# Latent attention and mLSTM of the odd layer: who computes the norms, in which order, and with which waits

## The reference, cut to what matters

```python
def odd_mixer(hn, positions, w_in, b_gate, g_qa, g_kva, w_q_up, w_kv_up, g_q, g_k, g_mh, w_out):
    z = hn @ w_in                       # 1024 -> 2216 columns
    q_lat, kv_lat, k_pe, mq, mk, mv, mo, mi, mf = jnp.split(z, ...)
    y_c = latent_attention(...)         # 8 heads, 64 content + 32 rotary columns, values 64
    h_m = mlstm_chunkwise(mq, mk, mv, mi + b_gate[:4], mf + b_gate[4:])   # 4 heads, 64, values 128
    y_d = sigmoid(mo) * rmsnorm(h_m, g_mh).reshape(...)
    return jnp.concatenate([y_c, y_d], -1) @ w_out

# in latent_attention: each head of q and of k is normed, content and rotary part separately
q = (rmsnorm(q_lat, g_qa) @ w_q_up);  kv = (rmsnorm(kv_lat, g_kva) @ w_kv_up)
q_nope = rmsnorm(q[..., :64], g_q[:64]); q_pe = rope(rmsnorm(q[..., 64:], g_q[64:]))
k_nope = rmsnorm(k_nope, g_k[:64]);      k_pe = rope(rmsnorm(k_pe, g_k[64:]))
```

## Time and profile before

| | |
|---|---|
| runs, us | 1380.41, 1379.68, 1378.28 (median 1379.68) |
| the profiled execution, us | 1380.87, its span 1379.0 |
| busy share of the span | PE 92%, DVE 55%, ACT 35%, POOL 2% |
| mean granted TensorE clock | 0.961 of 2.4 GHz |
| odd mixer | about 353 to 512 us of the span |

### The profile page before, as it was taken

How to read it: one execution, slowest core, us unless ns; L and a number is a source line. 1 busy time by engine, 2 the same in 40 slices (tenths; PEclk the granted TensorE clock), 3 DMA queues, 4 the chain that set the end, 5 groups by cost and what they waited for, 6 DMA issues and landing times.

```text
span 1379.0 us, 16368 instructions
## 1 busy us (share of the span) xinstructions
PE 1262.5 (92%) x6228; PEld 884.1 (64%) x6228; DVE 760.9 (55%) x1450; ACT 482.7 (35%) x806; POOL 27.0 (2%) x60
## 2 busy tenths in 40 slices
PE   6979999999896889999987998789999999999996
PEld 5967888876774667888875996554544454444442
DVE  5765877785657667777775998632122212222122
ACT  4424444444544335444444653411111111111111
POOL 0000000000000000000000300000000000000000
PEclk9989999999997689999999999889999999999999
DMA  8447766653421227777534320399999999999994
GB/s 272 149 153 287 268 244 244 243 183 137 169 95 51 92 87 285 267 254 254 194 110 150 122 77 1 150 424 418 414 432 427 429 432 431 431 429 429 432 430 186
DMA packets 113020, 354.42 MB, mean 257 GB/s; under 512 B 6762, under 2 KB 62755, under 8 KB 96578
## 3 DMA queue, kind: packets, MB, share of 16 engines
q1 hardware_dynamic: 106626, 328.48, 60.8%
q0 software_dynamic: 6336, 25.17, 4.6%
HBM read 352.58 MB, written 1.05 MB: 256 GB/s over the span
## 4 chain that ended last, share of the span: by engine, by line
PE 76%; DVE 10%; DMA 7%; ACT 3%; SPq 2%; issue 1%; DVEq 0%; ACTq 0%
PE ps L401 14%; PE ps L403 13%; PE ps L402 13%; PE ps L2538 13%; PE ps L2569 7%; PE ps L2527 4%; PE ps L2036 3%; DMA dense_weights<-in_moe_w_up 2%; DMA third_gate_up<-in_moe_w_up 2%; DMA second_expert<-in_moe_w_up 2%; DVE w_lo L375 1%; SPq L1053 1%; DMA dense_weights<-in_ev_w_in 1%; PE ps L2583 1%; PE ps L962 1%
## 5 line engine op out<-in xcount | busy, mean ns | idle before, releaser
L375 DVE TENSOR_TENSOR w_lo<-dense_weights,w_hi 128x1024 fp32r<-128x1024 f32 (+1 forms) x228 | 273.1, 1212 | 122.3 <-ACT w_hi L370 121.6
L370 ACT CAST w_hi<-dense_weights 128x1024 fp32r<-128x1024 f32 (+1 forms) x228 | 234.5, 1042 | 260.1 <-PE ps L403 236.3
L401 PE MATMUL ps<-w_hi,xT_lo 128*128 128x512 f32 (+1 forms) x624 | 251.1, 402 | 22.1 <-DVE xT_lo L2187 6.0
L403 PE MATMUL ps<-w_hi,xT_hi 128*128 128x512 f32 (+1 forms) x624 | 245.2, 393 | 0.0
L402 PE MATMUL ps<-w_lo,xT_hi 128*128 128x512 f32 (+1 forms) x624 | 245.1, 393 | 0.0
L401 PEld LDWEIGHTS ps<-w_hi,xT_lo 128*128 128x128 f32 x624 | 119.9, 192 | 51.1 <-issue 13.6
L403 PEld LDWEIGHTS ps<-w_hi,xT_hi 128*128 128x128 f32 x624 | 119.6, 192 | 25.4
L402 PEld LDWEIGHTS ps<-w_lo,xT_hi 128*128 128x128 f32 x624 | 120.2, 193 | 24.4 <-issue 0.7
L2676 DVE TENSOR_TENSOR hnT<-ps,g_bc 128x512 f32<-128x512 f32 x32 | 22.1, 692 | 163.5 <-PE ps L2569 163.5
L2685 DVE SCALAR_TENSOR_TENSOR cmask<-ge_th,ps 128x256 f32<-128x256 f32 x32 | 13.5, 422 | 163.0 <-ACT ge_th L2627 163.0
L2627 ACT ACTIVATE ge_th<-ps 128x256 f32<-128x256 f32 x32 | 12.3, 385 | 202.3 <-PE ps L2538 202.3
(11 more groups left out here) (404 smaller groups left out, 1778.0 us busy)
## 6 DMA issues: line engine op xcount, KB each, us to landing
ada_w<-in_ada_w POOLq DMA_DIRECT2D x12, 2048.0 KB, 12.2
dense_weights<-in_w_gate SPq DMA_DIRECT2D x22, 1024.0 KB, 7.1
dense_weights<-in_w_up SPq DMA_DIRECT2D x22, 1024.0 KB, 9.4
dense_weights<-in_w_down SPq DMA_DIRECT2D x22, 1024.0 KB, 5.0
dense_weights<-in_moe_w_gate SPq DMA_DIRECT2D x11, 2048.0 KB, 18.5
dense_weights<-in_moe_w_up SPq DMA_DIRECT2D x11, 2048.0 KB, 22.9
dense_weights<-in_moe_w_down SPq DMA_DIRECT2D x11, 2048.0 KB, 18.4
second_expert<-in_moe_w_gate SPq DMA_DIRECT2D x11, 2048.0 KB, 17.3
```

Of the source, the lines that this page charges most:

```text
L370: act.copy(split_view(w_hi, name, i, j), piece(name, i, j)).then_inc(hi_ready, 1)
L375: dve.tensor_tensor(split_view(w_lo, name, i, j), piece(name, i, j), split_view(w_hi, name, i, j).bitcast(F32), ALU.subtract).then_inc(pie ...
L401: pe.matmul(out, left[1], right[0], start=start, stop=False)
L403: return pe.matmul(out, left[0], right[0], start=False, stop=stop)
```

## The change

Nothing that is computed changes in the reference's sense; who does it, and when, does.

- Both barriers (`stage_end`, at the end of `OddHeads` and of `OddAttend`) are gone; named semaphores stand in for them (`act_copied`, `dve_copied`, `turned`).
- The factors of q and their multiplications move from after `scaled(4)` to before it (`q_factors`).
- Keys: ScalarE squares each quarter of kv out of PSUM with the factor 1/64 in its scale, and copies it; VectorE sums four quarters, takes one root, and multiplies once. The gain of the keys is applied when the turned keys are copied out, as a scale per partition (`gk_col`, made by three operations at the start of `OddIn`). ScalarE copies the rotary parts.
- TensorE turns the memory's q and k before it makes kv, and counts kv up by quarters.
- ScalarE loads the table for the exponential early, with a one-element operation.
- Gate sums: TensorE makes them between turned q and turned k, VectorE makes the columns before it copies turned keys.
- The mLSTM weights are made two operations after each of heads 4 to 7. The values' copy goes to ScalarE, the tanh before the last four copies.
- The turned attention half is moved into the last steps of `OddAttend`; the division has four operations instead of six; the mLSTM norm's squares are summed by ScalarE head by head; root and gate are applied in one operation per head and tile (eight).

```diff
@@ OddIn.dve
                 own(dve.tensor_tensor(g_k[:, 0:NOPE], g_k[:, 0:NOPE], g_q[:, 0:NOPE], ALU.mult))
+                wide = probT[:, 0, 0:QK]
+                own(dve.tensor_tensor(wide[:, 0:NOPE], ident[:, 0:NOPE], g_k[:, 0:NOPE], ALU.mult))
+                own(dve.tensor_copy(wide[:, NOPE:], ident[:, NOPE:QK]))
+                own(dve.tensor_reduce(gk_col, wide, AX.X, ALU.add))
                 self.up.turns_of(dve, own, self.freq)
...
                 split_upto(dve, split_lo, "od_in", 4, 3, 0)
+                odd_heads.q_factors(dve, own)
                 scaled(4)
@@ OddUp.act
+                act.wait_ge(self.mqk_turned, 1)
+                act.copy(mqkT[:], ps[:, 2:4, :].rearrange("p b (c s) -> p (b c) s", c=2)).then_inc(self.mqk_freed, 1)
...
-                act.wait_ge(up_used, 1)
-                act.copy(od_kv[:].rearrange("p t h d -> p t (h d)").rearrange("p t (a b) -> p (t a) b", a=2),
-                         ps[:, 4:8, :]).then_inc(self.kv_copied, 1)
...
+                for t in range(T):
+                    key = act.copy(od_k[:, t, :, NOPE:], od_z[:, t, AT_KPE:AT_KPE + ROPE].unsqueeze(1).to_broadcast([P, HEADS, ROPE]))
+                key.then_inc(self.exps, 1)
+                act.activation(turns[:, 0, 0:1], lf[:, 0, 0, 0:1], ACT.Exp)
+                for g in range(4):
+                    t, heads = g // 2, slice(g % 2 * (HEADS // 2), (g % 2 + 1) * (HEADS // 2))
+                    made = ps[:, 4 + g, :].rearrange("p (h d) -> p h d", h=HEADS // 2)
+                    act.wait_ge(up_used, g + 1)
+                    act.activation(od_k[:, t, heads, 0:NOPE], made[:, :, 0:NOPE], ACT.Square, scale=float(NOPE) ** -0.5
+                                   ).then_inc(self.kv_copied, 1)
+                    act.copy(od_kv[:, t, heads, :], made).then_inc(self.kv_copied, 1)
@@ OddHeads
+                for g in range(4):
+                    dve.wait_ge(self.up.kv_copied, 2 * g + 1)
...
+                    own(dve.tensor_reduce(ms[:, at:at + HEADS // 2], od_k[:, g // 2, half, 0:NOPE], AX.X, ALU.add))
+                rsqrt(dve, own, ms[:, cut], rs[:, cut], rtmp[:, 0, cut], rtmp[:, 1, cut])
+                dve.wait_ge(self.up.kv_copied, 8)
+                dve.tensor_tensor(k3[:, :, 0:NOPE], kv3[:, :, 0:NOPE], self.per_head(2 * n, NOPE), ALU.mult).then_inc(self.k_ready, 1)
+                odd_attend.gate_columns(dve, own)
...
+            def act(self, act):
+                for b in (0, 1, 2, 3, 5, 7):
+                    if b == 5:
+                        split_upto(act, split_hi, "od_out", 0, 3, ahead=0)
+                    act.wait_ge(self.turned, b + 1)
...
-                stage_end(pe)
@@ OddAttend
+                    if step == self.N:
+                        for b in range(2):
+                            odd_out.turn(pe, b)
...
+                    if hd >= HEADS - MH:
+                        memory_weights(hd - (HEADS - MH))
+                odd_out.gate(act)
                 for hd in range(HEADS, self.N):
                     copy(hd)
-                stage_end(act)
...
+                odd_out.gains(dve, own)
                 for m in range(MH):
+                    if m == 3:
+                        for b in range(2):
+                            odd_out.low(dve, b)
...
-                    own(dve.tensor_copy(den[:, 0], num[:, :, MV]))
-                    own(dve.tensor_scalar(den[:, 1], den[:, 0], -1.0, None, ALU.mult))
-                    own(dve.tensor_tensor(den[:, 0], den[:, 0], den[:, 1], ALU.max))
-                    own(dve.tensor_tensor(den[:, 0], den[:, 0], emt[:, :, m], ALU.max))
+                    own(dve.tensor_tensor(den[:, 0], num[:, :, MV], emt[:, :, m], ALU.max))
+                    own(dve.scalar_tensor_tensor(out=den[:, 0], in0=num[:, :, MV], scalar=-1.0, in1=den[:, 0], op0=ALU.mult, op1=ALU.max))
@@ OddOut
+                for m in range(MH):
+                    act.wait_ge(odd_attend.y_freed, T + m + 1)
+                    for t in range(T):
+                        act.activation(junk[:, t, m], y_d[:, t, m, :], ACT.Square, scale=float(MV) ** -0.5,
+                                       accum_out=ms[:, t * MH + m:t * MH + m + 1]).then_inc(self.tanh, 1)
...
+                for m in range(MH):
+                    for t in range(T):
+                        last = dve.scalar_tensor_tensor(out=y_d[:, t, m, :], in0=y_d[:, t, m, :], scalar=rs[:, t * MH + m:t * MH + m + 1],
+                                                        in1=g[:, t, m, :], op0=ALU.mult, op1=ALU.mult)
+                    if m % 2 == 1:
+                        last.then_inc(self.y, 1)
```

More of the change, by code:

```diff
@@ L1607, in dve @@
-                stage_end(dve)
-            def act(self, act):
-                for b in range(1, 8, 2):
-                    act.wait_ge(self.turned, b + 1)
-                    dst = (qT if b < 4 else kT)[0:QK, 2 * (b % 4):2 * (b % 4) + 2, :]
-                    act.copy(dst, ps[0:QK, b, :].rearrange("p (h s) -> p h s", h=2))
-                stage_end(act)
+                cut = slice(2 * n, 3 * n)
+                for g in range(4):
+                    dve.wait_ge(self.up.kv_copied, 2 * g + 1)
+                    at, half = 2 * n + g * (HEADS // 2), slice(g % 2 * (HEADS // 2), (g % 2 + 1) * (HEADS // 2))
+                    own(dve.tensor_reduce(ms[:, at:at + HEADS // 2], od_k[:, g // 2, half, 0:NOPE], AX.X, ALU.add))
@@ L1848, in act, with gate, gains @@
+            def gate(self, act):
+                act.activation(od_z[:, :, self.gains_at], od_z[:, :, AT_MO:AT_MI], ACT.Tanh, scale=0.5).then_inc(self.tanh, 1)
+            def gains(self, dve, own):
+                dve.wait_ge(self.tanh, 1)
+                g = od_z[:, :, self.gains_at]
+                own(dve.scalar_tensor_tensor(out=g, in0=g, scalar=1.0, in1=g_mh[:].unsqueeze(1).to_broadcast([P, T, MH * MV]),
+                                             op0=ALU.add, op1=ALU.mult))
             def act(self, act):
-                mo = od_z[:, :, AT_MO:AT_MI]
@@ L1891, in dve, with turn @@
                         ins.then_inc(h_ready, 1)
[L1893 to L1900 removed]
+            def turn(self, pe, b):
+                for c in (2 * b, 2 * b + 1):
+                    for t in range(T):
+                        at = (c % 2) * S + t * P
+                        last = pe.transpose(ps[:, b, at:at + P], mix[:, t, c * P:(c + 1) * P], ident[:])
+                last.then_inc(self.turned, 1)
+            def pe(self, pe):
                 def rest():
[L1904 to L1905 removed]
+                    for b in (2, 3):
+                        pe.wait_ge(self.y, b - 1)
+                        self.turn(pe, b)
                     pe.wait_ge(self.lo, 4)
[L1908 removed]
                 pe.wait_ge(self.lo, 2)
@@ L2820, in _ @@
             odd_in.pool(pool)
-            for _ in range(2):
-                stage_end(pool)
             ada_loads(pool, 1)
```

201 lines of the change are left out of this document (85 added, 116 removed).

## The result

The changed kernel takes 1371.26 us (median of 5, 1369.76 to 1371.75), the kernel before 1379.68 on the same chip (5, 1378.28 to 1381.89): ratio 0.9926, 95% interval 0.9908 to 0.9943: a gain under 1%, but the interval leaves out 1. The forecast was 1370.1 with a range of 1365.0 to 1375.0. The profiled execution took 1370.21 us, its span 1368.5, so 10.5 us less span than before.

What follows compares the result with a forecast made beforehand. It saw three bounds in turn: VectorE's and ScalarE's chain to the first exponential, a slow-TensorE head loop, a tail waiting for VectorE. Terms -0.8 + 5.4 + 0.7 + 2.2 + 1.2 + 0.9 = 9.6 us gave 1370.1, range 1365.0 to 1375.0.

Steps and rivals of the forecast that it cites:

- steps 1 and 4: Three new operations starting `OddIn`, 0.8 us lost; head 8's transposes to `OddOut`'s first product, 2.2 us saved.
- the second part of 3: From head 4's exponential to head 8's transposes: weights without a lump, 0.7 us saved, between -0.3 and 1.4.
- Start of `OddIn`: Three new VectorE operations lengthen TensorE's wait for piece 3's low part: 0.8 us lost, 0.6 to 1.9.
- Way to the first exponential: Query factors move into VectorE's idle time, VectorE then waits for ScalarE's squares: 5.4 us saved, 4.0 to 6.7.
- Heads: Nothing changes from the first exponential to head 4's; from there to head 8's transposes 0.7 us saved.
- End of the heads: From head 8's transposes to `OddOut`'s first product, 17.5 us becomes 15.2: 2.2 us saved, 1.5 to 4.
- The wait in the first block: TensorE's 1.19 us wait in `OddOut` for the gated half disappears: 1.2 us saved, at least 0.5.
- The clock: Shorter gaps around `OddOut` win back part of the 3.1 us lost to TensorE's lower clock: 0.9 us saved.
- Rival A: TensorE's clock stays down through all heads: 5.8 us saved, median 1373.9; chance 0.20.
- Rival B: The gap at 363 us grows, the clock stays down in `OddIn`: up to 9 us slower, 1388.5; chance 0.05.
- Rival C: The experts' weight stream, behind the odd mixer, swallows the gain: median 1379.5; chance 0.07.
- Rival D: The clock comes up in the heads: 14.3 us saved, median 1365.4; chance 0.08.

Runs made afterwards that it cites:

- e1: Changed kernel with the three operations that make the key gains' column moved from the start of `OddIn` to before the squares of q: 1366.08 us, ratio 0.990.
- e2: Changed kernel with the query factors put back behind the last scaled part, `scaled(4)`: 1369.48 us, ratio 0.9932.
- e3: Changed kernel with the one-element Exp that loads ScalarE's table moved from ahead of the key squares to behind the copy of `v_aug`: 1366.38 us, ratio 0.9895.
- e5: Changed kernel with unread TensorE transposes added ahead of the keys and through all heads: 1358.45 us, ratio 0.9842.
- e9: Kernel before the change with unread transposes added in all TensorE's waits in its heads and `OddOut`: 1370.15 us, ratio 0.9934.
- e11: The changed kernel run once more, unedited: 1368.21 us, ratio 0.9924.
- e8: Changed kernel with the mLSTM weights of the four memory heads made in one lump behind head 6's copy, as before the change: 1367.49 us, one run.
- e6: Changed kernel with `OddOut`'s normalisation back on VectorE, and the gains' product and ScalarE's tanh, all behind the heads: 1375.93 us, ratio 0.9971.
- e10: e1, e3 and e5 together on the changed kernel, with the turns' angles and sines moved behind `OddIn`'s first block: 1353.11 us, ratio 0.9811.
- e4: Changed kernel with 22 unread TensorE transposes added ahead of the keys and 14 ahead of head 0's turn: 1363.68 us, ratio 0.9881.

## Why the prediction was right

The time was right, 1.2 us from the median, and steps 1 and 4 and the second part of 3 were within 0.15 us. Errors of both signs stood in the others.

1. **Start of `OddIn`**, 0.8 lost: 0.72, and 0.70 won back in e1. Right in place and size.
2. **Way to the first exponential**, 5.4 saved: 6.7. The mechanism was right (VectorE waits for ScalarE's squares; e2 and e3 moved each side). The mis-sized term is the four square-and-copy pairs: 4.0 us predicted, from the nearest rows with their lengths added, and 2.95 measured (421.44 to 424.39), 0.74 a pair, since neighbouring operations overlap in the timeline: the copy starts 0.27 after the start of a square of 0.45. The pairs also began 0.5 sooner than worked out (6.95 us behind ScalarE's `scaled(4)`, not 7.44), and 0.4 of that went again at the last sum, which ends 0.2 behind the pairs and not before them. The rest fitted: from turned keys to the exponential 2.8 saved by the working, 2.9 measured. The row decided against the Trainium skill's sum for a table switch (ScalarE: Activation LUTs, "What ACT_TABLE_LOAD costs"): its 1.28 us of load show in e3, its 1.38 us of drain do not, since the operation behind the load starts 0.01 us later.
3. **Heads.** "From the first exponential to head 4's (...) nothing changes" failed: 2.6 lost. What sets this stretch is not the order (at a held clock both kernels take 10.56 us, e5 and e9) but when the clock rises, and that differs by 6.6 us between executions of one program (e11), worth 2.8. Behind head 4 0.7 was forecast, 0.84 came, and e8 took it back.
4. **End of the heads**, 17.5 to 15.2 us: 15.21. Right in size; no run puts its order back alone. At a held clock the same stretch is 14.22 us in e9 and 10.89 in e5.
5. **The wait in the first block**, 1.2 saved: the wait is gone. In the old order the second pair of transposes starts 8.89 us behind `OddOut`'s first product where the first half runs in part at the lower clock, and 9.99 (e6) or 8.86 (e9) where it runs at the upper one. VectorE's chain sets this, and not TensorE: in e9 its last operation ends 8.74 us behind the first product. Now they start after 5.57.
6. **The clock**, 0.9 of 3.1: the whole of it came. 5 and 6 together were 2.1 and are 4.7 us: 3.3 up to these transposes (8.89 to 5.57) and 1.4 behind them (9.77 to 8.39). The term of 0.9 was mis-sized because it treated the clock as coming back in part. Nor do the two steps add up as separate terms: the first half's 2 us of clock reach the path only because the wait is gone too.

So errors of +1.3, -2.6 and +2.6 us in steps 2, 3 and 5 with 6; another 1.7 went behind the mixer and 1.0 came from ahead of it. The agreement of the sum is in part luck. At a held clock (e5 against e9) the change is worth 12.6 to 13.05 us up to `h`, more than the 9.6 forecast and the 10.5 measured.

Rival A (clock down in all heads, 1373.9) had the right mechanism: the clock is at 0.50 from 452 to 476 us, but `OddOut` has it back. Rival B is out: the gap grew to 2.51 and the clock was back after nine products (363.00 to 366.7 us), though e10, which closes the gap, gains 1.7 us beside its 2.5. Rival C: 1.7 us are lost behind the mixer, 1.35 of them over one dip of the clock; that leaves 0.36 without a shown cause, and little for the weight stream. Rival D (the clock up in the heads) did not happen by itself; e5 makes it happen, and its size there is 9 to 12 us, about twice the 4.7 it was given beyond the forecast or more.

## What to carry to other kernels

Where the granted clock moves within a stretch, first see the stretch at a held clock (independent matrix work in TensorE's waits did that here, e4 and e5), and then judge an order. Here the held clock brought 9 us on the kernel before (e9) and 9 to 12 on the changed one (e5), and the order 8 to 10 without it and 12 to 13 with it: each was worth more with the other. When work leaves one engine's path, compute how late the next engine is: 5.2 us taken off VectorE were worth 1.1 at the keys because ScalarE stood behind it (e2), and the "early" table load cost 1.65 us until it stood where ScalarE idled (e3). A small block put at a stage's start is best checked against an idle stretch of the same engine later on.

## What was not expected of the hardware

- One program, two executions, the first exponential 77.8 us behind the g_k product in both, and the granted clock rises 10.6 us after it in one and 4.0 in the other (windows in e11). Behind `OddOut` it falls in eight of the twelve traces of the changed order (the changed kernel's own two and e10 among them) and not in the other four, with the same work there.
- 36 added transposes cost no time that shows and took 4.1 us off heads 0 to 3 against one execution of the changed kernel and 1.3 against the other (e4). In the same 6.70 us TensorE was busy 100% at a granted 0.54, and 70% at 0.99.
- ScalarE's operations on 256 and 512 columns of one bank start 0.27 us and 0.47 us apart though they are listed with 0.45 and 0.65: a pair takes 0.74 us, two thirds of the sum of its listed lengths.
